# Down-projection weights of twelve expert pairs issued from ScalarE's queue instead of SyncE's

## The reference

```python
def hier_moe(h, w_rg, b_rg, w_re, b_re, w_g, w_u, w_d):
    # top-1 of 4 groups, then top-2 of the 8 experts in it -> combine (T, 32)
    ...
        a = jnp.einsum('cd,edf->cef', tc, w_g)      # gate, per expert 1024 x 256
        u = jnp.einsum('cd,edf->cef', tc, w_u)      # up,   per expert 1024 x 256
        z = jax.nn.silu(a) * u * cc[..., None].astype(tc.dtype)
        return jnp.einsum('cef,efd->cd', z, w_d)    # down, per expert 256 x 1024
    ...
x = x + hier_moe(rms_norm(x, ffn_norm_g[l]), ...)
```

## Time and profile before

| what | value |
|---|---|
| three executions | 1293.31, 1296.68, 1297.34 us (median 1296.68) |
| the profiled execution | 1295.96 us, its span 1294.1 us |
| mean granted TensorE clock | 0.977 |
| PE busy | 1196.4 us, 92% |
| ACT busy | 410.2 us, 32% |
| moved on SP's queue (q1) | 282.98 MB |
| moved on ACT's queue (q10) | 0.77 MB |

### The profile page before, as it was taken

How to read it: one execution, slowest core, us unless ns; L and a number is a source line. 1 busy time by engine, 2 the same in 40 slices (tenths; PEclk the granted TensorE clock), 3 DMA queues, 4 the chain that set the end, 5 groups by cost and what they waited for, 6 DMA issues and landing times.

```text
span 1294.1 us, 17654 instructions
## 1 busy us (share of the span) xinstructions
PE 1196.4 (92%) x6456; PEld 798.6 (62%) x6456; DVE 590.2 (46%) x1420; ACT 410.2 (32%) x818; POOL 242.8 (19%) x179
## 2 busy tenths in 40 slices
PE   7999998999999999889599999989999999988881
PEld 6777787888886344223287777778888853433320
DVE  4667864434445232112456778553344442222115
ACT  5444456333342111001244444563333411110002
POOL 1405420222200111111022344102221001111100
PEclk9999999999999999889799999999999999999897
DMA  5333321563667999999833333126537779999995
GB/s 206 114 82 99 106 76 34 211 210 98 229 232 281 393 421 422 426 421 411 330 95 92 86 113 104 34 93 221 174 98 294 247 272 413 422 422 424 418 411 224
DMA packets 74432, 306.03 MB, mean 236 GB/s; under 512 B 12214, under 2 KB 12598, under 8 KB 65648
## 3 DMA queue, kind: packets, MB, share of 16 engines
q1 hardware_dynamic: 63760, 282.98, 58.6%
q0 software_dynamic: 10304, 21.23, 4.3%
q10 hardware_dynamic: 288, 0.77, 0.2%
HBM read 289.16 MB, written 23.07 MB: 241 GB/s over the span
## 4 chain that ended last, share of the span: by engine, by line
PE 69%; DMA 13%; SPq 8%; DVE 4%; ACT 3%; issue 2%; DVEq 1%; POOLq 0%; ACTq 0%
PE bank L605 14%; PE bank L607 14%; PE bank L606 14%; PE bank L946 9%; DMA gu<-in_gu_w 9%; PE bank L962 5%; SPq L431 5%; SPq L436 3%; PE bank L735 2%; PE bank L764 2%; PE bank L699 1%; DMA raw<-in_stream 1%; PE bank L933 1%; PE bank L868 1%; ACT prob L1172 1%
## 5 line engine op out<-in xcount | busy, mean ns | idle before, releaser
L946 PE MATMUL bank<-gu,xgt 128*64 128x512 f32 x968 | 228.2, 618 | 31.8 <-DMA gu<-in_gu_w 31.7
L605 PE MATMUL bank<-h_hi,w_hi 128*128 128x512 f32 x640 | 253.9, 397 | 2.7 <-DVE h_lo L1394 1.9
L607 PE MATMUL bank<-h_hi,w_lo 128*128 128x512 f32 x640 | 249.5, 390 | 0.0
L606 PE MATMUL bank<-h_lo,w_hi 128*128 128x512 f32 x640 | 249.1, 389 | 0.0
L1359 DVE TENSOR_TENSOR w_lo<-raw,w_hi 128x1024 fp32r<-128x1024 f32 x100 | 132.5, 1326 | 121.5 <-ACT w_hi L1082 121.5
L946 PEld LDWEIGHTS bank<-gu,xgt 128*64 128x64 f32 x968 | 70.6, 142 | 182.8 <-issue 141.3
L605 PEld LDWEIGHTS bank<-h_hi,w_hi 128*128 128x128 f32 x640 | 120.2, 188 | 28.5 <-issue 3.3
L607 PEld LDWEIGHTS bank<-h_hi,w_lo 128*128 128x128 f32 x640 | 120.1, 188 | 25.6
L606 PEld LDWEIGHTS bank<-h_lo,w_hi 128*128 128x128 f32 x640 | 120.3, 188 | 23.6
L962 PE MATMUL bank<-dn,zt 128*64 128x512 f32 x512 | 117.3, 599 | 6.1 <-ACT zt L1316 2.8
L1082 ACT ACTIVATE w_hi<-raw 128x1024 fp32r<-128x1024 f32 x100 | 105.3, 1053 | 46.3 <-PE bank L607 42.8
(11 more groups left out here) (210 smaller groups left out, 1671.3 us busy)
## 6 DMA issues: line engine op xcount, KB each, us to landing
raw<-in_stream SPq DMA_DIRECT2D x112, 512.0 KB, 3.6
gu<-in_gu_w SPq DMA_DIRECT2D x12, 4096.0 KB, 35.5
gu<-in_gu_w SPq DMA_DIRECT2D x40, 1024.0 KB, 14.1
dn<-in_dn_w SPq DMA_DIRECT2D x32, 1024.0 KB, 14.1
dn<-in_dn_w SPq DMA_DIRECT2D x12, 2048.0 KB, 36.1
gu<-in_gu_w SPq DMA_DIRECT2D x34, 512.0 KB, 5.4
gu<-in_gu_w SPq DMA_DIRECT2D x8, 2048.0 KB, 26.6
swp<-pj SPq DMA_DIRECT2D x136, 64.0 KB, 2.7
```

Source lines behind the costliest of these rows:

```text
L605: mm(dst, ah, bh, start=start, stop=False)
L606: mm(dst, ah, bl, start=False, stop=False)
L607: return mm(dst, al, bh, start=False, stop=stop)
L946: last = mm(bank[b][e * CAP:(e + 1) * CAP, :], xgt[:, x_s, k, e * CAP:(e + 1) * CAP], gate_up(n, w_s, e, k), start=k == 0, stop=k == KD - 1)
```

## The change

The down weights of pairs 4 to 15 of each layer are no longer issued by SP. ScalarE issues them: behind its copy of pair n's half of the result (L1310) it issues `dn` of pair n + 3, for n from 1 to 12. The condition for the slot is the same (`dn_ok` of pair n), and the sizes and pieces are the same. SP's loop holds only the gate and up weights and their waits.

```diff
@@ SyncE's loop over p from 4 to 15
                     else:
                         load_gu(l, p)
-                    sp.wait_ge(dn_ok, l * PAIRS + p - RING + 1)
-                    if p in PARTS:
-                        load_dn_part(l, p, 0)
-                        load_dn_part(l, p, 1)
-                    else:
-                        load_dn(l, p)
@@ ScalarE
+                def load_dn(l, p):
+
+                    s = p % RING
+                    act.wait_ge(dn_ok, l * PAIRS + p - RING + 1)
+                    if p in PARTS:
+                        for f in range(2):
+                            act.dma_start(dn[s][:, :, f, :], dn_w[bass.ds(l * PAIRS + p, 1), :, :, f * D:(f + 1) * D].rearrange(
+                                "o e p n -> p (o e) n")).then_inc(dn_part[p][f], 16)
+                    else:
+                        act.dma_start(dn[s][:, :, :, :].rearrange("p e k n -> p e (k n)"),
+                                      dn_w[bass.ds(l * PAIRS + p, 1), :, :, :].rearrange("o e p n -> p (o e) n")).then_inc(dn_ld[s], 16)
+
...
                     y_half(n)
+                    if 4 <= n + RING < PAIRS:
+                        load_dn(l, n + RING)
```

More of the change, by code:

```diff
@@ L422, in load_gu @@
                              gu_w[bass.ds(l * PAIRS + p, 1), :, :, :].rearrange("o e p n -> p (o e) n")).then_inc(gu_ld[s], 16)
[L424 to L427, removed]
             def load_gu_part(l, p, q):
```

## The result

The changed kernel takes 1305.91 us (median of 5 runs, 1305.83 to 1310.08) against 1296.68 us before; the ratio is 1.0086 (95% interval 1.0075 to 1.0097). So it is 11 us slower by the ratio (9.7 to 12.6), while the two medians lie 9.2 us apart. The profiled execution took 1308.22 us, its span 1306.3 us. It lies 2.3 us above the median, so lengths that are read from its trace are a little longer than the ratio says. Forecast were 1309 us, 12.6 us more than before, and a range of 1300 to 1318.

What follows compares the result with a forecast made beforehand. The prediction took full DMA engines moving fixed bytes as the bound. All terms were 0 except byte order at each layer's end: 1295.96 + 2 x 6.3 = 1308.6 us profiled, 1309 us as median, range 1300 to 1318.

Steps and rivals of the forecast that it cites:

- What bounds the stage: Expert stage: DMA engines have no gap (share 1.02), so a fixed number of bytes leaves at a fixed pace.
- (a): SP's queue: removing twelve waits for `dn_ok` and 18 issues per layer gains 0.
- (b): ACT's queue: one or two added issues per pair, 0.41 us each, covered by 6.27 us idle; cost 0.
- that rival: ACT stands in the issue of late pairs' loads as SP did, delaying silu; 1318 us, chance 0.12.
- the step on the scatter: Copies on ACT: scatters get a smaller share, but even 5 us more stays inside PE's 8.7 us; cost 0.
- (c): End of each layer: down weights arrive early, so `gu` 15 comes last; 6.3 us per layer, 12.6 in all.
- the first bound: Layer's end: last `gu` 15 quarter lands at 1267.2, plus 7.5 us of PE work; 5.1 us later than before.
- the second bound: Layer's end: PE has 20.0 us of work after the last `gu` 14 quarter lands; 6.3 us later than before.
- (d): PE's tail in each layer may run partly at the lower clock after a wait: 0 to 2.9 us, taken as 0.
- The pace term: Full stretches: two load queues might gain 4.6 us or lose 2.9 us per layer; taken as 0.
- What to look for: Signs listed for the profile after: where `dn` and `gu` land, DMA share, GB/s, PE's waits and end.
- at least a third of the pace: `dn` on ACT's queue, served beside other queues: 2.1 MB at 140 GB/s takes 15 us, about one pair.

Runs made afterwards that it cites:

- but15_act: Kernel before, with down weights of pairs 4 to 14 issued by ScalarE and pair 15's left on the load queue; 1295.78 us, ratio 1.0000.
- middle_act: Kernel before, with down weights of pairs 4 to 12 issued by ScalarE and 13 to 15 left on the load queue; 1297.2 us, ratio 1.0001.
- tail_act: Kernel before, with down weights of pairs 13, 14 and 15 alone issued by ScalarE; 1309.03 us, ratio 1.0089.
- only15_act: Kernel before, with only the down weights of pair 15 issued by ScalarE; 1305.87 us, ratio 1.0071.
- swap15_sp: Kernel before, one load queue, with pair 15's down weights issued ahead of its gate and up weights; 1305.96 us, ratio 1.0066.
- ahead_sp: Kernel before, one load queue, with down weights of pairs 14 and 15 issued ahead of pair 14's gate and up weights; 1308.55 us, ratio 1.0095.
- small_rows_sp: Kernel before, one load queue, with whole-slot loads of pairs 7 to 12 cut to 4 KB rows; 1304.12 us, ratio 1.0059.

## Why the prediction was right, and which steps were not

**What bounds the stage** (full DMA engines, a fixed number of bytes): right. SP's issues were gone from the chain that ended last (8% of the span before, 0% after; the longest still took 8.8 us), and nothing was gained. but15_act shows it best: its chain holds 0% of them too, and its ratio is 1.0000.

**(a) Removed waits and issues at 0:** right. middle_act and but15_act take 9 and 11 of the 12 waits per layer out of SP's loop and measure 1.0001 and 1.0000.

**(b) Added issues on ACT at 0:** right in price. They took 0.37 to 0.44 us each at the median, 1.3 us at most; ACT was not held as SP had been, and that rival falls. The sign that was named for it, a silu over 0.1 us behind its up part, did come, but from the copies ahead of the silu and not from the issues. But the step on the scatter was wrong in size, as the prediction put it: "even 5 us more would stay inside the 8.7 us". The scatters took 14.6 us more (29.0 for 14.4), the copies waited up to 15.2 us, silu and z were late behind them, and PE waited for z, 4.33 us at 509.94 and 35.1 us in twelve waits. The total stayed right because these waits took the place of those for `gu`: PE's idle time ahead of its up parts that `gu` ended was 31.7 us over the span and is now 5.8 us. The prediction had said of waits for `gu` that they cost nothing in the middle, and had not thought of these, so that the zero held for them too is in part luck. A wait in the middle only decides which link holds PE, while the engines stay full. middle_act shows it by its time.

**(c) The order of the bytes:** right, and shown in five ways (tail_act, only15_act, swap15_sp, ahead_sp dear; middle_act free). The sizes: the first bound, 5.1 us, measured 4.3 to 4.6 per layer (swap15_sp, only15_act). The second was 6.3 us, with a tail of 20.0 us from the landing of the last `gu` quarter of 14. It measured 6.7 and 5.9 us in the trace, and 5.6 us per layer by the ratio of all runs. The quarter landed 1 to 2 us earlier than worked out: the last quarter of 15 landed at 627.3 where about 628 was forecast, and the four quarters of 15 took 11.7 us, the figure of the earlier trace rows, for the 11.3 taken. The tail was 21.4 us long in layer one and 21.3 in layer two. One inner step was too simple: "all down weights are in before gu 15 starts" is not enough for the second bound. In only15_act they are in, but those of pair 14 come between `gu` 14 and `gu` 15, so the last quarter of 14 is there earlier (611.82 for 615.70 in the changed kernel) and PE keeps pace. The second bound needs the down weights of pair 14 ahead of the end of `gu` 14 too, as ahead_sp and the changed kernel have them.

**(d) Clock at 0:** wrong by 1.1 to 1.6 us per layer, inside the 0 to 2.9 that the range kept. The last quarter of 14 took 3.51 and 3.06 us for 1.94, behind waits of 3.64 and 2.20 us. The table by stretches around it in layer one:

```profile
612.00:616.00 4.00, 0.36 (x4) 0.20 (x4) 0.00 (x0) 0.00 (x0) 0.00 (x0) 0.99 1.03 416
616.00:620.00 4.00, 4.00 (x15) 1.36 (x12) 0.34 (x1) 0.38 (x1) 0.00 (x0) 0.58 1.03 413
620.00:624.00 4.00, 3.53 (x19) 1.32 (x19) 1.37 (x3) 0.38 (x1) 0.00 (x0) 1.00 0.92 368
```

PE is idle nearly all of 612 to 616 us, and in the next 4 us the granted clock is 0.58, most of that stretch at 1.2 GHz; then it is back at 2.4. The last two columns show the load engines beginning to run dry from 620 us on, with 17 us of PE's work left. The slow quarter used up about what the earlier landing had gained. Two terms were off and nearly cancelled; that the sum per layer came so near is in this part luck.

**The pace term at 0:** right, 416, 425 and 423 GB/s up to 580 us for 416, 423 and 423. The rule from the Trainium skill, "DMA: Bandwidth & Descriptors", section "Rules for kernel authors" (spreading doesn't add bandwidth), says the same, and the trace agrees: both load queues had work here and the pace moved by at most 2 GB/s in 425.

**What to look for:** `dn` on ACT's queue was to land in 10 to 17 us; the whole-slot loads took 27.7. The "at least a third of the pace", 140 GB/s, was a third of the turns, but 30% of the bytes: 10.33 MB in 80 us, 129 GB/s. That makes 16 us for 2.1 MB; the rest of the 27.7 is time behind the load before it on the same queue. Whole pairs' down weights therefore ran ahead by less than two pairs, still enough. PE's first wait was to be for `gu` at pair 7 or 8; it was for z, at pair 6.

Left open: why but15_act loses nothing measurable, though its last quarter of 14 lands about 5 us later. In the trace its last down part is 1.1 us later in layer one and 0.3 us in layer two; the estimate was 1 to 2 per layer, and the timing allows at most 0.9.

## What to carry to other kernels

Where the DMA engines are full from start to end, ask which bytes come last and how much work hangs on them; the order of the last few transfers was worth more here than any issue time or wait in the middle. A single queue keeps that order, and a second queue gives it up without moving more. A long wait in a profile, even 342 us in total, is not shown to be a cost until an experiment takes it away and the time follows.

## What the runs showed of the hardware

- Three queues with work took equal turns by packets, whatever a packet's size: 1368, 1363 and 1367 packets of 15.4, 7.6 and 1.8 KB in 80 us of the changed kernel, and 1367, 1367 and 1365 in the same stretch of middle_act. The Trainium skill, "DMA: Bandwidth & Descriptors", section "Queues, rings and completion order", says that each engine goes round the queues at packet granularity; these counts agree.
- So long packets in the load queues starve a queue of short ones. GpSimd's gathers and scatters landed in 10.2 and 14.4 us beside one load queue of 16 and 8 KB rows, in 22.1 and 29.0 us beside two, in 8.3 and 10.2 us beside two whose rows are 4 KB, and in 7.2 and 8.0 us beside one of 4 KB rows (small_rows_sp).
- Weights in 1 MB transfers with rows of 4 KB moved at 410 to 411 GB/s, in transfers of 4 and 2 MB with rows of 16 and 8 KB at 423 to 425, with the engines' share at 1.0 in both. Doubling the rows of the down weights alone added 1 to 3 GB/s in its one trace.
- Loads issued from two queues together moved what one did: 416, 425 and 423 GB/s for 416, 423 and 423.
